# Gate projection of the sparse half put ahead of the first sparse pair's transposes and exponentials

## Chip, cores and metric

The kernel runs on one core of one Trainium2 chip. The metric is the device time of one execution in microseconds (us). In the profile PE is TensorE (PEld its weight loads), ACT ScalarE, DVE VectorE, POOL GpSimd, and SP the engine that issues the plain DMAs.

## What is computed

The reference is a first block (mixers, cross attention, and a feed-forward layer that looks up single-neuron experts) followed by two layers of a second block. All of what is changed lies in the second block:

```python
def hybrid_layer(x, w_in, w_out, ln_g, ln_b, rel_bias, topk):
    proj = jnp.einsum('bsd,dn->bsn', x, w_in)
    qA, kA, vA, gA, qB, kB, vB, gB, qI, kI, wI = jnp.split(proj, SPLIT_POINTS, axis=-1)
    oA = stick_breaking_attention(heads(qA), heads(kA), heads(vA))
    oB = dsa_sparse_attention(heads(qB), heads(kB), heads(vB), qI, kI, wI, rel_bias, topk)
    mix = jnp.concatenate([oA * jax.nn.silu(gA), oB * jax.nn.silu(gB)], axis=-1)
    y = jnp.einsum('bsm,md->bsd', mix, w_out)
    return layer_norm(ALPHA * x + y, ln_g, ln_b)
```

The sequence has 512 tokens of width 1024. Each half (A, the "stick" half, and B, the "sparse" half) has 8 heads of width 64. `gB` is the gate projection of the sparse half: a 1024 by 512 product for each token. The expert look-up of the first block gathers 16 rows for each of 8 heads of each token, and each row is dotted with the token, passed through a GELU, and added.

## The kernel before

The second block is run in three groups of query tiles of 128 tokens: group 0 has tiles 0 and 1, group 1 has tile 2, group 2 has tile 3. Each group goes through both layers, so there are six passes. In the trace they lie at 1630 to 1900 and 1900 to 2165 us (group 0), 2165 to 2430 and 2430 to 2690 us (group 1), and 2690 to 2850 and 2850 to 3013 us (group 2). What comes before 1630 us is the first block.

Beside the passes of groups 0 and 1 runs the background work: the expert look-up for the tokens of the next group, 128 rows for each of the two groups. A row is one gather into one of 10 slots, issued by POOL (L1335, about 1 MB for the 128 tokens), a dot product on DVE (L2438, 1.2 us), and a scaled addition on DVE (L2452, 1.3 us). Four rows make a lot. A lot's GELU (L2252) runs on ACT once its four dots are there, with an activation table load before it and one after it (1.28 us each). DVE multiplies the result by the gate weights (L2444, "weigh") before it adds the rows of the lot, five rows behind the dots. Which rows are done where is fixed: the code of DVE and ACT has named points between its steps (`rows(point)`, `gelus(point)`), and a list of weights, `layer_points`, says how many rows are due at each. From it follow, for the points around the change:

- group 0 layer 0: GELU of lot 9 at the point ("g1", 0), of lot 10 at ("gate1"), of lot 11 at ("sparse", 0, 2). DVE weighs lot 9 in its rows of ("g1", 1) and lot 10 in those of ("gate1").
- group 0 layer 1: GELU of lot 26 at ("gate1"), weighed by DVE in its rows of ("gate1").
- group 1 layer 0: GELU of lot 10 at ("g1", 2), weighed in ("gate1").
- group 1 layer 1: GELU of lot 26 at ("gate1"), weighed in ("gate1").
- group 2 has no background work.

Each engine carries out its program in order and waits on semaphores. A pass has 8 head pairs u: 0 to 3 stick, 4 to 7 sparse. `pair(l, u)` projects queries and keys (L78, weights from the ring), `natural` projects gates or values for a whole half (L2082, 16 matmul instructions of 512 columns for each tile). For a sparse pair, `sparse_logits` (L2159) is followed by `shift` on DVE (L2572: adds the bias, and takes the maximum), `sparse_weights` on ACT (L2350: exponentials, one for each head and tile), `turn_weights` on PE (L2167: transposes), `copy_turned` on ACT (L2357) and `sparse_out` on PE (L78). `gates` on ACT handles a tile's gate projection in four operations: copy, exponential, logarithm, exponential (L2334, L2335, L2337, L2339). `turn_mix` (L2191) and `copy_mix` (L2362) turn the finished half of the mix. Projections share two PSUM banks in turn, so that `pair(l, 6)` waits for the first `copy_mix` of the stick half.

Weights come through a ring of 6 blocks of 512 KB, loaded by SP in the order of use (L1874): ..., v1 (4 blocks), pair 5 (2), g1 (4), pair 6 (2), pair 7 (2), out (8). A block's load waits until the block six before it has been used: the g1 blocks wait for the value projection v1 and need nothing later. Behind the load that waits for g1, SP issues the bias of the third sparse pair (`load_bias(l, 2)`, L1919), which waits also for the first `shift`, and behind the loads that wait for pair 6 the bias of the fourth. POOL adds the mask to each bias (`add_keep`, L2001) before its `shift`.

Of the kernel before, what the change touches and what calls it, by code (L numbers as in the profile page):

```python
# [26 lines left out]
PAIRS = HEADS // 2  # L27
# [1634 lines left out]
STICK, SPARSE = 0, 1  # L1662
# [117 lines left out]
def group_stage(nc, A, m, number, out):  # L1780
# [8 lines left out]
    tiles = GROUPS[number]  # L1789
# [27 lines left out]
    with ctx:  # L1817
# [36 lines left out]
        with nc.Block() as block:  # L1854
# [165 lines left out]
            def _(pe):  # L2020
                def start(job):
                    n = job_at[job]
                    if n >= 2:
                        pe.wait_ge(proj_copied, n - 1)
                    return ps[:, n % 2, :]
# [50 lines left out]
                def natural(l, name, half):  # L2076
                    for t in tiles:
                        bank = start((l, f"{name}{half}", t))
                        for b in range(4):
                            w = weights_of(l, half, name, b)  # L2080
                            for c in range(2):
                                made = nc.tensor.matmul(bank, x_t[:, 2 * b + c, local(t)], w[:, c * HALF:(c + 1) * HALF],  # L2082
                                                        start=b == 0 and c == 0, stop=b == 3 and c == 1)
                        made.then_inc(proj_done, 1)

                def pair(l, u):
                    bank = start((l, "pair", u))
                    for k, name in enumerate("qk"):
                        made = turned_product(bank[:, k * NQ:(k + 1) * NQ], weights_of(l, u // PAIRS, name, u % PAIRS))
                    made.then_inc(proj_done, 1)  # L2090
# [72 lines left out]
                def turn_weights(l, u):  # L2163
                    pe.wait_ge(prob_ready, PAIRS * l + u - PAIRS + 1)
                    for e in range(2):
                        for b in range(SC // P):
                            made = nc.tensor.transpose(ps[:, pair_banks(u) + e, b * P:(b + 1) * P], work[:, u % 2, e, b * P:(b + 1) * P], m.ident[:, :])  # L2167
                    made.then_inc(turned, 1)
# [38 lines left out]
                for l in range(LAYERS):  # L2207
                    for t in tiles:
                        for n in range(2):
                            turn_input(l, t, n)  # L2210
                    copied(("x", last, 1) if l == 0 else (l - 1, "x", last, 1))
                    index_keys(l)
                    index_queries(l, 0)
                    index_queries(l, 1)
                    natural(l, "v", STICK)
                    index_scores(l)
                    pair(l, 0)
                    stick_logits(l, 0)
                    natural(l, "g", STICK)
                    for u in range(PAIRS):  # L2220
                        pair(l, u + 1)
                        tails(l, u)
                        if u + 1 < PAIRS:
                            stick_logits(l, u + 1)
                        else:
                            natural(l, "v", SPARSE)
                            sparse_logits(l, PAIRS)
                        stick_out(l, u)
                    for u in range(PAIRS, UNITS):
                        if u + 1 < UNITS:  # L2230
                            pair(l, u + 1)
                        turn_weights(l, u)
                        if u + 1 < UNITS:
                            sparse_logits(l, u + 1)
                        if u == PAIRS:
                            natural(l, "g", SPARSE)
                        sparse_out(l, u)
                        if u == PAIRS:
                            turn_mix(l, STICK)
                    turn_mix(l, SPARSE)  # L2240
                    output(l)

            @block.scalar
            def _(act):
# [77 lines left out]
                        act.wait_ge(attended, UNITS * l + u)  # L2322
                    nc.scalar.activation(work[:, 1, :, :], ps[:, pair_banks(u):pair_banks(u) + 2, 0:SC], ACT.Exp).then_inc(weighted, 1)

                def gates(l, half, done):

                    if half == STICK and searched:
                        act.wait_ge(summed, SCORES * (l + 1))
                    if half == SPARSE:
                        act.wait_ge(gate_ready, NT * (2 * l + 1))  # L2330
                    for n, t in enumerate(tiles):
                        count = NT * (2 * l + half) + n
                        bank = finished((l, f"g{half}", t))
                        nc.scalar.activation(mix[:, n, half * HALF:(half + 1) * HALF], bank, ACT.Copy)  # L2334
                        nc.scalar.activation(share[:, n, :], bank, ACT.Exp, scale=-1.0).then_inc(proj_copied, 1)  # L2335
                        act.wait_ge(proj_copied, job_at[l, f"g{half}", t] + 1)
                        nc.scalar.activation(share[:, n, :], share[:, n, :], ACT.Ln, bias=1.0).then_inc(gate_step, 1)  # L2337
                        act.wait_ge(gate_step, 2 * count + 1)
                        nc.scalar.activation(share[:, n, :], share[:, n, :], ACT.Exp, scale=-1.0).then_inc(gate_step, 1)  # L2339
                        done = gelus((l, f"g{half}", t), done)  # L2340
                    return done

                def sparse_weights(l, u):
                    n = PAIRS * l + u - PAIRS
# [20 lines left out]
                done = 0  # L2365
# [4 lines left out]
                done = gelus((0, "first"), done)  # L2370
                inverse_roots(0)
                for l in range(LAYERS):
                    done = gelus((l, "first"), done)
                    for t in tiles:
                        for n in range(2):
                            copy_input(l, t, n)
                    done = gelus((l, "start"), done)
                    copy_index_keys(l)
                    done = gelus((l, "kI"), done)
                    for n in range(2):  # L2380
                        copy_index_queries(l, n)
                        done = gelus((l, "qI", n), done)
                    done = copy_values(l, STICK, done)
                    for n in range(SCORES):
                        rectify(l, n)
                        if n % 2:
                            done = gelus((l, "scores", searched[n // HEADS], n % HEADS), done)
                    copy_pair(l, 0)
                    done = gelus((l, "pair0"), done)
                    softplus(l, 0)  # L2390
                    done = gelus((l, "soft0"), done)
                    done = gates(l, STICK, done)
                    for u in range(PAIRS):
                        copy_pair(l, u + 1)
                        done = gelus((l, "stick", u, 0), done)
                        stick_weights(l, u)
                        done = gelus((l, "stick", u, 1), done)
                        if u + 1 < PAIRS:
                            softplus(l, u + 1)
                        else:  # L2400
                            done = copy_values(l, SPARSE, done)
                        done = gelus((l, "stick", u, 2), done)
                        done = gelus((l, "stick", u, 3), done)
                    done = gelus((l, "keep"), done)
                    for u in range(PAIRS, UNITS):
                        p = u - PAIRS
                        if p == 0:
                            sparse_weights(l, u)
                            copy_pair(l, u + 1)
                            copy_turned(l, u)  # L2410
                            done = gates(l, SPARSE, done)
                            done = gelus((l, "gate1"), done)
                            copy_mix(l, STICK)
                        else:
                            sparse_weights(l, u)
                            done = gelus((l, "sparse", p, 0), done) if p else done
                            if u + 1 < UNITS:
                                copy_pair(l, u + 1)
                            copy_turned(l, u)
                        done = gelus((l, "sparse", p, 1), done)  # L2420
                        done = gelus((l, "sparse", p, 2), done)
                        done = gelus((l, "sparse", p, 3), done)
                    copy_mix(l, SPARSE)
                    done = gelus((l, "out"), done)
                    inverse_roots(l + 1)
                    done = gelus((l, "norm"), done)
# [355 lines left out]
```

## Time and profile before

| | |
|---|---|
| time, median of 3 runs | 3016.38 us (3012.67 to 3020.07) |
| the profiled execution: time, span | 3014.64 us, 3012.9 us |
| busy: PE, DVE, POOL, ACT | 81%, 58%, 32%, 30% of the span |
| gathers of expert rows (software queue) | 536.90 MB of 803.85 MB moved |
| TensorE clock granted, mean | 0.888 |

The profiled execution is 1.7 us below the median. The busy shares are averages over stages that have different limits: the passes of groups 0 and 1 have the gathers and VectorE's rows beside them, those of group 2 have not. In a timeline row stand the start, the duration, engine, line, operation, output and inputs, and in brackets the idle time of the engine before it and what ended it. For DVE rows "issue" names a wait that the profile can't attribute.

### The profile page before, as it was taken

Reading aid. Unit: us, or ns where it says so; the run is one execution under the profiler, and the core shown is the slowest. Engines: PE = TensorE matmul, PEld = TensorE weight load, DVE = VectorE, ACT = ScalarE, POOL = GpSimd, SP = SyncE. Lnnn points to the kernel's source line nnn. Section 1 sums busy time; section 2 is a strip of 40 time slices with the busy share of each in tenths; the row PEclk is TensorE's granted clock in tenths of the full one; section 3 lists DMA queues with packets and bytes.
Section 4 is the critical chain, followed back from the end, with each engine's and each line's share of the span. In section 5 each row is a group of like instructions: output and inputs, shape, how many; then the busy total and the mean of one; then the engine's idle time right before and its main releaser. Section 6 shows DMA issues by size and latency. Waiting matters only on the chain. (4 is left out here: it accounts for less than half of the span.)

```text
span 3012.9 us, 30208 instructions
## 1 busy us (share of the span) xinstructions
PE 2428.3 (81%) x9721; PEld 1627.9 (54%) x9721; DVE 1743.7 (58%) x3652; ACT 905.9 (30%) x1730; POOL 979.0 (32%) x691
## 2 busy tenths in 40 slices
PE   6997999869876888889785996798557468559897
PEld 4776878758653343334333664575246336436674
DVE  3444311031128888988964687587669859855142
ACT  4444222223311222222222442244134324323232
POOL 2232554433302434343451234234213523410001
PEclk9998999979988999999897997898778677769899
DMA  4321333223118999999998899899789999964553
GB/s 159 94 66 49 98 105 97 101 71 108 56 39 330 392 418 409 411 412 403 403 416 351 320 366 369 331 355 402 277 342 382 413 400 373 390 269 157 215 185 138
DMA packets 255851, 803.85 MB, mean 267 GB/s; under 512 B 18302, under 2 KB 138518, under 8 KB 190183
## 3 DMA queue, kind: packets, MB, share of 16 engines
q0 software_dynamic: 73728, 536.90, 43.9%
q1 hardware_dynamic: 181991, 265.35, 25.3%
q8 instruction: 63, 1.03, 0.1%
q14 instruction: 69, 0.57, 0.0%
HBM read 793.36 MB, written 14.07 MB: 268 GB/s over the span
## 5 line engine op out<-in xcount | busy, mean ns | idle before, releaser
L1335 POOL DMA_INDIRECT gathered<-in_peer_rows,experts x436 | 530.6, 1217 | 928.8 <-DVE x_res L2452 630.7
L1446 PE MATMUL peer_banks<-gathered,peer_diags 128*128 128x512 f32 x720 | 342.8, 633 | 60.3 <-ACT peer_diags L1506 60.2
L78 PE MATMUL group_banks<-group_x_t,group_ring 128*128 128x128 f32 (+1 forms) x2016 | 340.2, 332 | 15.9 <-ACT group_x_t L2264 8.4
L2438 DVE CUSTOM_DVE_ANT_0 gathered<-gathered,late_nat 128x1024 f32<-128x1024 f32 x256 | 315.7, 1236 | 42.0 <-DMA gathered<-in_peer_rows,experts 29.0
L78 PEld LDWEIGHTS group_banks<-group_x_t,group_ring 128*128 128x128 f32 x2016 | 307.6, 208 | 46.0 <-ACT group_x_t L2264 10.8
L2452 DVE SCALAR_TENSOR_TENSOR x_res<-gathered,group_weights,x_res 128x1024 f32<-128x1024 f32 x256 | 329.8, 1288 | 2.5
L1446 PEld LDWEIGHTS peer_banks<-gathered,peer_diags 128*128 128x128 f32 x720 | 144.6, 204 | 249.5 <-issue 249.2
L2082 PE MATMUL group_banks<-group_ring,group_x_t 128*128 128x512 f32 x512 | 233.3, 610 | 28.2 <-DMA group_ring<-in_weights 28.2
L1609 DVE CUSTOM_DVE_ANT_0 peer_product<-gathered,early_nat 128x1024 f32<-128x1024 f32 x180 | 214.8, 1222 | 41.2 <-DMA gathered<-in_peer_rows,experts 41.1
L1446 PE MATMUL peer_banks<-peer_early_gathered,peer_diags 128*128 128x512 f32 x304 | 148.9, 643 | 45.9 <-ACT peer_diags L1506 45.9
L1499 ACT ACTIVATE peer_acts<-peer_dots 128x2 f32<-128x2 f32 x128 | 26.0, 203 | 518.1 <-DVE peer_dots L1609 517.9
L2082 PEld LDWEIGHTS group_banks<-group_ring,group_x_t 128*128 128x128 f32 x512 | 98.1, 197 | 150.0 <-issue 117.7
L2001 POOL TENSOR_TENSOR group_bias<-group_bias,group_keep 128x768 f32<-128x768 f32 (+1 forms) x24 | 48.9, 2049 | 342.9 <-DVE group_keep L2507 249.6
L1335 POOL DMA_INDIRECT peer_early_gathered<-in_peer_rows,experts x76 | 81.6, 1074 | 207.0 <-PE peer_banks L1446 119.1
L1446 PEld LDWEIGHTS peer_banks<-peer_early_gathered,peer_diags 128*128 128x128 f32 x304 | 61.9, 208 | 127.8 <-issue 127.8
L2167 PE MATMUL group_banks<-ident,group_work 128*128 128x128 f32 x160 | 30.0, 342 | 121.5 <-ACT group_work L2350 115.6
L2200 PE MATMUL group_banks<-group_ring,group_mix_t 128*128 128x512 f32 x256 | 123.7, 646 | 4.1 <-ACT group_mix_t L2362 4.1
L78 PE MATMUL peer_banks<-peer_h_t,peer_w 128*128 128x512 f32 x256 | 115.2, 605 | 8.0 <-DMA peer_w<-in_w_pq 8.0
L95 POOL TENSOR_TENSOR mixer_wq_parts<-mixer_wq,mixer_wq_parts 128x1024 fp32r<-128x1024 f32 x24 | 58.2, 2427 | 189.4 <-ACT mixer_wq_parts L526 121.9
L78 PEld LDWEIGHTS group_banks<-group_values,group_work 128*128 128x128 f32 x640 | 93.5, 229 | 24.1 <-ACT group_work L2357 16.9
L944 DVE TENSOR_TENSOR merge_gated<-merge_gates,merge_banks 128x512 f32<-128x512 f32 x16 | 11.0, 689 | 163.1 <-PE merge_banks L78 163.1
L2043 PE MATMUL group_banks<-ident,x_res 128*128 128x128 f32 x64 | 16.2, 427 | 107.2 <-DVE x_res L2476 81.4
(324 smaller groups left out, 4307.9 us busy)
## 6 DMA issues: line engine op xcount, KB each, us to landing
group_ring<-in_weights SPq DMA_DIRECT2D x270, 512.0 KB, 5.5
mixer_wq<-in_w_in SPq DMA_DIRECT2D x24, 512.0 KB, 4.4
mixer_wk<-in_w_in SPq DMA_DIRECT2D x24, 512.0 KB, 5.7
peer_w<-in_w_pq SPq DMA_DIRECT2D x8, 1024.0 KB
gathered<-in_peer_rows,experts POOLq DMA_INDIRECT x436
diff_wv<-in_w_in SPq DMA_DIRECT2D x8, 512.0 KB, 4.2
conv_wb<-in_w_in SPq DMA_DIRECT2D x8, 512.0 KB, 4.1
merge_w<-in_w_conv_out SPq DMA_DIRECT2D x8, 512.0 KB, 3.6
```

Source lines behind the costliest of these rows:

```text
L78: last = nc.tensor.matmul(out, lhsT, rhs, start=n == 0, stop=n == len(pairs) - 1)
L95: return engine.tensor_tensor(low, whole, high.bitcast(F32), ALU.subtract)
L1335: nc.gpsimd.indirect_dma_start(row_buffer(m, r), None, A["peer_rows"], bass.IndirectOffsetOnAxis(ap=at, axis=0))\
L1446: last = nc.tensor.matmul(ps[:, ACC[unit % 2] + half, :], diags[:, r % DIAGS, :], row_buffer(m, r)[:, D + half * BANK:D + (half + 1) * BAN ...
L1499: nc.scalar.activation(acts[:, lot % RING, :], dots[:, lot % RING, :], ACT.Gelu).then_inc(gelu_done, 1)
L1609: nc.vector.tensor_tensor_reduce(out=product[:, r % 2, :], in0=row_buffer(m, r)[:, 0:D], in1=nat[t // 2][:, t % 2, :], scale=1.0, scalar=0 ...
L2001: nc.gpsimd.tensor_tensor(bias[:, n % 2, :, :], bias[:, n % 2, :, :], keep[:, :].unsqueeze(1).to_broadcast([P, 2, SC]), ALU.add)\
L2082: made = nc.tensor.matmul(bank, x_t[:, 2 * b + c, local(t)], w[:, c * HALF:(c + 1) * HALF], start=b == 0 and c == 0, stop=b == 3 and c == 1)
L2167: made = nc.tensor.transpose(ps[:, pair_banks(u) + e, b * P:(b + 1) * P], work[:, u % 2, e, b * P:(b + 1) * P], m.ident[:, :])
L2200: made = nc.tensor.matmul(ps[:, 2 + 2 * n + half, :], mix_t[:, c, local(t)], w[:, half * HALF:(half + 1) * HALF], start=c == 0, stop=c == ...
L2438: nc.vector.tensor_tensor_reduce(out=row, in0=row, in1=m.late_nat[:, t % 2, :], scale=1.0, scalar=0.0, op0=ALU.mult, op1=ALU.add, accum_ou ...
L2452: nc.vector.scalar_tensor_tensor(out=m.x[:, t, :], in0=row_buffer(m, r)[:, D:2 * D], scalar=weights[:, lot % bg.RING, n % bg.LOT:n % bg.LO ...
```

## The change

In a pass, TensorE now runs the gate projection of the sparse half right after `pair(l, 5)`, before `turn_weights` of pair 4. ScalarE copies pair 5 and does the gates of all tiles before the exponentials of pair 4. `gates` no longer calls `gelus` behind each tile: for the stick half the calls follow behind the loop, and for the sparse half the GELUs due at ("g1", t) are done by the call for ("gate1"), behind `copy_turned` of pair 4. DVE, POOL and SP have the same programs as before.

```diff
                     for u in range(PAIRS, UNITS):
                         if u + 1 < UNITS:
                             pair(l, u + 1)
+                        if u == PAIRS:
+                            natural(l, "g", SPARSE)
                         turn_weights(l, u)
                         if u + 1 < UNITS:
                             sparse_logits(l, u + 1)
-                        if u == PAIRS:
-                            natural(l, "g", SPARSE)
                         sparse_out(l, u)
                         if u == PAIRS:
                             turn_mix(l, STICK)
@@
-                def gates(l, half, done):
+                def gates(l, half):
...
                         nc.scalar.activation(share[:, n, :], share[:, n, :], ACT.Exp, scale=-1.0).then_inc(gate_step, 1)
-                        done = gelus((l, f"g{half}", t), done)
-                    return done
@@
                     done = gelus((l, "soft0"), done)
-                    done = gates(l, STICK, done)
+                    gates(l, STICK)
+                    for t in tiles:
+                        done = gelus((l, "g0", t), done)
@@
                         if p == 0:
+                            copy_pair(l, u + 1)
+                            gates(l, SPARSE)
                             sparse_weights(l, u)
-                            copy_pair(l, u + 1)
                             copy_turned(l, u)
-                            done = gates(l, SPARSE, done)
                             done = gelus((l, "gate1"), done)
                             copy_mix(l, STICK)
```

## Rows read from the trace of the kernel before

**Rows 1.** Windows, one per pass; the last three columns are clock, DMA share, GB/s

```profile
1630.00:1900.00 270.00, 224.94 (x856) 153.18 (x856) 192.15 (x325) 91.90 (x157) 88.73 (x65) 0.88 0.92 354
...
2165.00:2430.00 265.00, 151.89 (x728) 108.96 (x728) 202.99 (x315) 85.27 (x131) 90.93 (x67) 0.75 0.92 363
...
2850.00:3013.00 163.00, 141.15 (x784) 100.94 (x784) 54.99 (x106) 44.49 (x80) 9.35 (x4) 0.93 0.45 167
```

**Rows 2.** Waits of VectorE in 1630 to 2690: us in total, times, longest

```profile
DVE group_weights L2444 <- ACT group_acts L2252: 64.0, 8, 21.0
...
DVE gathered L2438 <- DMA gathered<-in_peer_rows,experts: 29.0, 25, 2.9
```

**Rows 3.** Timeline, group 0 layer 0, first half

```profile
1782.84 0.40 ACT L2350 ACTIVATE group_work<-group_work,group_neg_top 128x128 f32<-128x128 f32 x1 [6.07 <-DVE group_neg_top L2572]
...
1784.76 0.88 PE L2167 MATMUL group_banks<-ident,group_work 128*128 128x128 f32 x6 [2.12 <-ACT group_work L2350]
...
1785.68 0.81 ACT L2357 ACTIVATE group_work<-group_banks 128x768 f32<-128x768 f32 x1 [0.44 <-PE group_banks L2167]
...
1792.02 8.85 PE L2082 MATMUL group_banks<-group_ring,group_x_t 128*128 128x512 f32 x20 [0.17 <-DMA group_ring<-in_weights]
...
1798.06 0.16 DVE L2444 TENSOR_TENSOR group_weights<-group_acts,gates 128x4 f32<-128x4 f32 x1 [7.33 <-ACT group_acts L2252]
...
1800.91 0.60 ACT L2334 ACTIVATE group_mix<-group_banks 128x512 f32<-128x512 f32 x1 [1.58 <-PE group_banks L2082]
...
1806.80 5.41 PE L78 MATMUL group_banks<-group_x_t,group_ring 128*128 128x256 f32 x16 [3.76 <-ACT group_mix_t L2362]
```

**Rows 4.** Timeline, group 0 layer 0, second half

```profile
1811.78 1.23 DVE L2438 CUSTOM_DVE_ANT_0 gathered<-gathered,late_nat 128x1024 f32<-128x1024 f32 x1 [2.64 <-DMA gathered<-in_peer_rows,experts]
...
1817.02 1.85 SPq L1919 DMA_DIRECT2D group_bias<-bias_table  x4
...
1842.84 1.80 POOL L2001 TENSOR_TENSOR group_bias<-group_bias,group_keep 128x768 f32<-128x768 f32 x1 [9.44 <-DMA group_bias<-bias_table]
...
1844.77 0.29 DVE L2572 CUSTOM_DVE_ANT_0 group_work<-group_banks,group_bias 128x128 f32<-128x128 f32 x1 [8.07 <-POOL group_bias L2001]
```

**Rows 5.** Timeline, group 0 layer 1

```profile
2055.33 0.88 PE L2167 MATMUL group_banks<-ident,group_work 128*128 128x128 f32 x6 [3.11 <-ACT group_work L2350]
...
2076.63 0.16 DVE L2444 TENSOR_TENSOR group_weights<-group_acts,gates 128x4 f32<-128x4 f32 x1 [7.68 <-ACT group_acts L2252]
```

**Rows 6.** DMA issues, 2043 to 2054, median us to landing

```profile
group_ring<-in_weights SPq DMA_DIRECT2D x6, 512.0 KB, 18.9
```

**Rows 7.** Windows, group 0 layer 1, columns as in Rows 1

```profile
2055.30:2059.30 4.00, 3.97 (x16) 2.42 (x17) 3.96 (x8) 1.32 (x3) 1.21 (x1) 0.61 1.01 417
```

**Rows 8.** Timeline, group 1 layer 0

```profile
2344.18 1.54 PE L2167 MATMUL group_banks<-ident,group_work 128*128 128x128 f32 x6 [16.27 <-ACT group_work L2350]
...
2359.64 0.16 DVE L2444 TENSOR_TENSOR group_weights<-group_acts,gates 128x4 f32<-128x4 f32 x1 [3.79 <-ACT group_acts L2252]
```

**Rows 9.** Timeline, group 1 layer 1

```profile
2606.69 0.16 DVE L2444 TENSOR_TENSOR group_weights<-group_acts,gates 128x4 f32<-128x4 f32 x1 [3.83 <-ACT group_acts L2252]
```

**Rows 10.** Timeline, group 2 layer 1

```profile
2944.45 0.72 ACT L2350 ACTIVATE group_work<-group_work,group_neg_top 128x512 f32<-128x512 f32 x1 [1.21 <-DVE group_neg_top L2572]
...
2945.79 0.19 ACT L2350 ACTIVATION_READ_ACCUMULATOR group_work<-group_work,group_neg_top 128x1 f32 x1
...
2958.32 0.60 ACT L2334 ACTIVATE group_mix<-group_banks 128x512 f32<-128x512 f32 x1 [7.16 <-PE group_banks L2082]
...
2960.10 0.63 ACT L2339 ACTIVATE group_share<-group_share 128x512 f32<-128x512 f32 x1
...
2972.74 1.09 PE L2167 MATMUL group_banks<-ident,group_work 128*128 128x128 f32 x8 [1.16 <-ACT group_work L2350]
...
2975.15 0.69 DVE L2572 CUSTOM_DVE_ANT_0 group_work<-group_banks,group_bias 128x512 f32<-128x512 f32 x1 [3.40 <-PE group_banks L2159]
```

**Rows 11.** Timeline, group 2 layer 0

```profile
2815.25 1.09 PE L2167 MATMUL group_banks<-ident,group_work 128*128 128x128 f32 x8 [1.07 <-ACT group_work L2350]
```

## The prediction

> **What bounds the kernel now.** I read the passes one by one first. In the four passes of groups 0 and 1 TensorE is busy for 152 to 225 of some 265 us, VectorE for 192 to 203, and the DMA engines for about 0.9 of the time at 350 to 360 GB/s; in the two of group 2 TensorE is busy for 141 of 163 us and the rest has room [rows 1]. So the same edit meets two machines. In groups 0 and 1 the chain runs mostly through VectorE, which has its rows in order between the steps of the pass, and behind it stand the gathers. VectorE's idle time there is the second view: 64.0 us in 8 waits go to GELU results (L2444), 29.0 us in 25 waits to gathers that have not landed [rows 2]. In group 2 TensorE's own program is the chain. The third view is the timeline around the moved work, pass by pass, and there the question is the same each time: what did TensorE do in the place where the gate projection (g1) is put, and who waits for ScalarE behind the gates.
>
> **The change, part by part.** No arithmetic is added or removed: g1 is 16 matmul instructions for each tile before and after. In group 0 layer 0, two table switches fall away because two lots' GELUs are now done in one call. ScalarE isn't short of time there, so this is costed at nothing; if it were, it is two loads of 1.28 us. The gates of the stick half do the same work in the same order in all six passes (the first tile of two has no lot due), so nothing.
>
> *Group 2, layer 1.* TensorE has no hole here: the exponentials of pair 4 end at 2944.45 to 2945.98 [rows 10], before pair 5 is through at about 2949, and the transposes follow without a wait. With the change g1 takes that place, and then the transposes wait for ScalarE, which now first does the gates: from g1's end to the first gate operation 0.26 us, the four gate operations 2.41 us (2958.32 to 2960.73), the exponentials 1.53 us, 0.05 us to TensorE [rows 10]. That is 4.25 us of new idle time. The copy of the transposes, once hidden under g1, is hidden under the next logits but for some 0.1 us. Given back: TensorE waited 1.16 us before the transposes of pair 6, because the third bias came late [rows 10]; that bias is now asked for some 2 us earlier, since g1 ends earlier, and TensorE comes 4.25 us later, so the wait goes. Net +3.1 us. What is late next is the fourth bias, which SP issues only when pair 6 is through, 4.25 us later; the last shift began at 2975.15 right behind it [rows 10]. If it lands as slowly as before, +4.3; it competes with fewer blocks, so I keep 3.1.
>
> *Group 2, layer 0.* Same pattern, with 1.07 us given back [rows 11]: +3.2 us. Bounds for each of the two passes: 1.7 (the last shift also had slack) and 4.3.
>
> *TensorE's clock in group 2.* In group 0 layer 1 TensorE idled 3.11 us before the transposes [rows 5], and in the 4 us behind it the granted clock was 0.61, so near the lower level of 1.2 GHz for most of it [rows 7]; that is 0.39 times 4 = 1.6 us lost. The new gap of 4.25 us is longer. I charge 1.6 us twice, 3.2 in all; bounds 0 (the gap falls well) and 6.4 (the low clock comes back later in the pass as well). The Trainium skill says in "TensorE: Matmul & The Clock Gate", section "HAM oscillation", that idle gaps of some length put the array back to the lower clock, so that the burst behind each gap starts slow. By that rule the whole of the 3.2 us is due, and without it nothing; the trace of group 0 layer 1 agrees with the rule.
>
> *Group 0, layer 0.* TensorE idled only 2.12 us before the transposes, and the last g1 block landed at 1792.02 [rows 3]. So g1 can start earlier but not end earlier: its first tile waits for the same block, and its second tile is through at 1800.7, as before. Now the order on ScalarE costs. Before, the GELU of lot 9 stood between the gates of the two tiles, and VectorE, which had waited for it for 7.33 us, went on at 1798.06 [rows 3]. After, it stands behind the gates of both tiles (1800.91 + 2.41 = 1803.3), the exponentials (1782.84 to 1784.76, so 1.92: 1805.2), transposes and their copy (1784.76 to 1786.49, so 1.73: 1807.0) [rows 3], and a table load and the GELU (1.5): 1808.5. VectorE goes on 10.5 us later. Behind it lot 10 must be done as well before `copy_mix`: two additions, two dots and a weigh, 5.2 us, then GELU and table load, so `copy_mix` comes at 1815.3 and pair 6 at about 1816 where it was at 1806.80 [rows 3]. VectorE gets back the 2.64 us that it waited for a gather: +7.9 on that road [rows 4]. But the fourth bias is issued behind pair 6 (at 1817.02), POOL waited 9.44 us for its landing, and VectorE 8.07 us for POOL [rows 4]: on that road +9.3. I take +9. Below 5 it can't well come, since both roads would have to be shortened by the DMA queues emptying during VectorE's longer stall; above, 10.5.
>
> *Group 0, layer 1.* One lot (26), which stands behind the gates in both orders, so only the exponentials, transposes and copy (1.92 + 1.73 = 3.7) are put ahead of it, less what g1 gains. TensorE idled 3.11 us [rows 5]. A block takes 18.9 us to land [rows 6]; the g1 blocks are issued at about 2044, so the last is there at about 2063, and g1 gains 1 to 2 us at most. Range −2.7 (blocks there at once) to +3.3; I take +2. VectorE waited 7.68 us for this lot [rows 5], so it is on the path.
>
> *Group 1, both layers.* Here is the hole that fits: TensorE idled 16.27 us before the transposes in layer 0 [rows 8] and about as long in layer 1, because the shift on VectorE is late. g1 fits into it, and the gates are done before the exponentials are asked for. But what follows is not TensorE's. The next exponentials wait for VectorE's rows; the only wait of VectorE that hangs on the moved work is that for a GELU behind the gates, 3.79 and 3.83 us [rows 8, 9]. It goes. In its place the gathers are late next: the DMA engines are at 0.92 of the pass [rows 1], and VectorE waits for gathers already [rows 2]. I take half, −2 in each pass; bounds 0 and −3.8.
>
> **Sum.** 9 + 2 − 2 − 2 + 3.1 + 3.2 + 3.2 = +16.5 us on the profiled execution's own 3014.6: 3031.1. The median before is 1.7 us above that execution. I leave the forecast at 3031.
>
> **Rivals.**
>
> *B, TensorE's holes are the gain.* g1 leaves TensorE's chain wherever it idled: 2.12 and 3.11 in group 0 [rows 3, 5], and g1's whole length of about 7.5 us in each pass of group 1 [rows 8]. With group 2 at no cost that is −20, 2996 us. For it: the holes are real, and waits for exponentials end them. Against: behind them VectorE's rows, not TensorE, end the next wait. It decides if in group 1 the shift of pair 5 turns out to wait for its logits, and not to stand behind rows. This is the one that ends on the other side.
>
> *C, the loss is absorbed.* The delays of group 0 fall to the lower bounds (5 and −2.7), since queues that emptied deliver faster, group 1 gives its full 7.6, and group 2 costs 2 × 1.7 with no slow clock: 5 − 2.7 − 7.6 + 3.4 = −1.9, and half way to the forecast it is +7. So 3013 to 3023, about no change. For it: in the trace VectorE has 29 us of gather waits that a late VectorE would not meet. Against: only the 2.64 us lies close behind the delay in group 0.
>
> *D, the low clock spreads.* Upper bounds: 10.5 + 3.3 + 0 + 8.6 + 6.4 = +29, 3044 us. For it: TensorE gets new gaps in four passes. Against: the clock came back within 4 us behind the gap that I can see.
>
> **How the numbers follow.** No change within 0.3% (about what a measurement of this kernel can tell apart) is within 9 us of 3016.4. Chances: forecast 0.50, C 0.24, D 0.20, B 0.06. So slower 0.70, the same 0.24, faster 0.06. The range reaches from the upper part of C to most of D: 3016 to 3043.
>
> **What the profile after would show.** Right: in group 2 an idle time of about 4.2 us before the first transposes of pair 4, ended by ScalarE; no wait before those of pair 6; in group 0 layer 0 VectorE waiting about 18 us for the GELU of lot 9 where it waited 7.33; in group 1 the waits of 3.8 us at L2444 gone, with more waiting for gathers, and the waits of 16 us before the transposes smaller by g1. Wrong: if group 1's passes are shorter by more than 4 us each, VectorE was not their bound; if group 0 layer 0 is not longer, the GELU's place doesn't matter; if group 2 is not longer, ScalarE's gates overlap something that I took for serial.

## The result and the profile after

The changed kernel takes 3028.62 us (median of 6 runs, 3023.45 to 3035.45), the kernel before 3018.2 us (median of 6, 3012.67 to 3022.36). The ratio is 1.004, with a 95% interval of 1.0027 to 1.0052: slower by 12 us (10.4 us by the medians alone), and 8 to 16 us are in the interval. Further down, one execution of e6 is left out of its ratio: it took 3267.69 us at a mean granted clock of 0.76, the others of that kernel had 0.88 to 0.89. The profiled execution took 3027.14 us, with a span of 3025.4 us where the one before had 3012.9. The first lines of its page, engines and then the queue of the gathers, hardly differ from before: the work is the same, and 12.5 us more are waits and work at a lower clock. The mean granted clock doesn't show it (0.891 after, 0.888 before).

```profile
PE 2431.9 (80%) x9721; PEld 1632.8 (54%) x9721; DVE 1746.1 (58%) x3652; ACT 903.6 (30%) x1728; POOL 987.5 (33%) x691
...
q0 software_dynamic: 73728, 536.90, 43.8%
```

**Group 2.** This is the timeline of layer 1 after, which answers to [rows 10].

```profile
2950.85 7.03 PE L2082 MATMUL group_banks<-group_ring,group_x_t 128*128 128x512 f32 x16
...
2957.98 0.60 ACT L2334 ACTIVATE group_mix<-group_banks 128x512 f32<-128x512 f32 x1 [6.48 <-PE group_banks L2082]
...
2961.85 1.27 PE L2167 MATMUL group_banks<-ident,group_work 128*128 128x128 f32 x8 [3.97 <-ACT group_work L2348]
...
2963.05 2.08 PE L2159 MATMUL group_banks<-group_k_t,group_q_t 64*128 64x512 f32 x4
...
2965.06 3.68 PE L78 MATMUL group_banks<-group_values,group_work 128*128 128x64 f32 x16
...
2967.20 2.36 POOL L2001 TENSOR_TENSOR group_bias<-group_bias,group_keep 128x1024 f32<-128x1024 f32 x1 [21.50 <-DMA group_bias<-bias_table]
...
2969.38 5.41 PE L78 MATMUL group_banks<-group_x_t,group_ring 128*128 128x128 f32 x32
...
2974.62 1.04 PE L2167 MATMUL group_banks<-ident,group_work 128*128 128x128 f32 x8
...
2982.23 1.04 PE L2167 MATMUL group_banks<-ident,group_work 128*128 128x128 f32 x8
...
2987.57 1.09 PE L2167 MATMUL group_banks<-ident,group_work 128*128 128x128 f32 x8 [1.19 <-ACT group_work L2348]
```

The projection runs from 2950.85 to 2957.9. ScalarE's gates start at 2957.98, and the transposes of pair 4 begin at 2961.85 after 3.97 us of idle time (forecast 4.25). POOL has the third bias ready at 2969.6, and the transposes of pair 6 (2982.23) no longer wait. Those of pair 7 (2987.57) wait 1.19 us, though, where they waited 0.51 before:

```profile
2977.46 1.09 PE L2167 MATMUL group_banks<-ident,group_work 128*128 128x128 f32 x8 [0.51 <-ACT group_work L2350]
```

This is the fourth bias, which the prediction had named as late next: POOL has it ready at 2985.14, and the last shift begins at 2985.26. So in layer 1 some 0.7 of the 1.16 us given back are taken again. Layer 0 has the same pattern up to pair 6: 3.97 us before the transposes at 2801.20, none before those at 2821.60. There the last wait went down, from 1.76 to 0.32 us.

What the reader should look at are the durations in between: logits 2.08 us where they take 1.13 at full clock, the product 3.68 for 2.00, the projection of pair 6 5.41 for 3.79. The windows of the same stretch say why (columns as in Rows 1, the clock third from the end):

```profile
2954.00:2957.90 3.90, 3.88 (x10) 1.38 (x8) 0.00 (x0) 0.00 (x0) 0.00 (x0) 1.00 0.39 152
2961.80:2967.00 5.20, 5.15 (x21) 3.33 (x22) 1.82 (x5) 1.02 (x1) 0.00 (x0) 0.58 0.78 307
2967.00:2974.60 7.60, 7.60 (x45) 7.60 (x45) 0.09 (x1) 2.00 (x5) 2.36 (x1) 0.61 0.00 1
```

From the first transposes to those of pair 5 it is 12.77 us after (2961.85 to 2974.62). In the trace before, the same stretch was 14.75 us with the projection in it (from 2949.06 to 2963.81), so 7.78 without its 6.97. The 5.0 us on top are work at or near the lower clock of 1.2 GHz, but for the 0.3 us of copy that is no longer hidden (e4 below has 8.06 us for the same stretch at full clock).

**Group 0, layer 0.** The same rows as in [rows 3]:

```profile
1779.71 14.16 PE L2082 MATMUL group_banks<-group_ring,group_x_t 128*128 128x512 f32 x32
...
1793.90 0.60 ACT L2334 ACTIVATE group_mix<-group_banks 128x512 f32<-128x512 f32 x1 [4.40 <-PE group_banks L2082]
...
1798.12 1.04 PE L2167 MATMUL group_banks<-ident,group_work 128*128 128x128 f32 x6 [4.25 <-ACT group_work L2348]
...
1801.55 0.16 DVE L2444 TENSOR_TENSOR group_weights<-group_acts,gates 128x4 f32<-128x4 f32 x1 [11.59 <-ACT group_acts L2252]
...
1808.72 8.95 PE L78 MATMUL group_banks<-group_x_t,group_ring 128*128 128x256 f32 x32 [3.52 <-ACT group_mix_t L2360]
```

The projection of both tiles runs from 1779.71 to 1793.87 without a stop of its own. The fourth block did land only when TensorE came to it: its first weight load waited for it (0.82 us, of which the products lost at most 0.3: the row takes 14.16 us, and 13.90 in e4 and e9).

```profile
1785.01 0.19 PEld L2082 LDWEIGHTS group_banks<-group_ring,group_x_t 128*128 128x128 f32 x1 [0.82 <-DMA group_ring<-in_weights]
```

I had taken the landing at 1792.02 in [rows 3] for a fixed time. Measured from the end of the value projection, which frees the ring (1773.3 before, 1770.5 after), the block was there after 18.8 us in the trace before and after 14.5 us in this one. So the projection is over 4.2 us earlier than before by the same measure, and VectorE's wait at L2444 is 11.59 us, not the 18 us forecast, where it was 7.33. The landing differs from trace to trace. These are from e3, then e8 (below), which have TensorE's new order in group 0 as well:

```profile
1788.85 8.85 PE L2082 MATMUL group_banks<-group_ring,group_x_t 128*128 128x512 f32 x20 [1.79 <-DMA group_ring<-in_weights]
```

```profile
1789.91 8.85 PE L2082 MATMUL group_banks<-group_ring,group_x_t 128*128 128x512 f32 x20 [1.80 <-DMA group_ring<-in_weights]
```

There the block came 17.8 and 16.8 us after the value projection, and TensorE stood still for the ring for 3.0 and 2.0 us in all. In e4 and e9 it didn't wait.

The trace before was also not typical in the place where the projection was put. Of six traces whose code is as before in group 0 (before, e1, e2, e5, e6, e10), two have a hole of 2.1 us before the first transposes, and four have one of 4.1 us, as e1, whose wait for the GELU of lot 9 comes second:

```profile
1780.16 0.88 PE L2167 MATMUL group_banks<-ident,group_work 128*128 128x128 f32 x6 [4.10 <-ACT group_work L2353]
...
1794.65 0.16 DVE L2453 TENSOR_TENSOR group_weights<-group_acts,gates 128x4 f32<-128x4 f32 x1 [8.52 <-ACT group_acts L2254]
```

The logits behind this hole run slowly (1.63 us where they took 0.93), and the projection ends 30.8 us after the value projection, not 27.6 as in the trace before. Against such an execution the new place of the projection gains 7.4 us, not 4.2.

**Group 1.** Waits of VectorE over both passes; before (2164.4 to 2678.6 us) first:

```profile
DVE group_weights L2444 <- ACT group_acts L2252: 28.7, 3, 21.0
DVE gathered L2438 <- DMA gathered<-in_peer_rows,experts: 23.7, 20, 2.9
```

and after (2167 to 2677.1 us):

```profile
DVE gathered L2438 <- DMA gathered<-in_peer_rows,experts: 26.5, 29, 2.7
DVE group_weights L2444 <- ACT group_acts L2252: 22.5, 1, 22.5
```

Two of the three waits for a GELU (3.79 and 3.83 us) are gone, as forecast, and 9 more short waits for gathers stand in their place. And the projection did not simply drop into the idle time: in layer 0 it had to wait for its own weights.

```profile
2333.76 7.08 PE L2082 MATMUL group_banks<-group_ring,group_x_t 128*128 128x512 f32 x12 [2.64 <-DMA group_ring<-in_weights]
...
2341.58 1.98 PE L2082 MATMUL group_banks<-group_ring,group_x_t 128*128 128x512 f32 x4 [0.73 <-DMA group_ring<-in_weights]
...
2347.50 0.88 PE L2167 MATMUL group_banks<-ident,group_work 128*128 128x128 f32 x6 [3.94 <-ACT group_work L2348]
...
2373.21 1.54 PE L2167 MATMUL group_banks<-ident,group_work 128*128 128x128 f32 x6 [15.30 <-ACT group_work L2348]
```

It stood still twice for the ring, ended at 2343.56, and the gates behind it held the transposes until 2347.50, where before they began at 2344.18 [rows 8] (the whole trace is 2.5 us later there). The transposes of pair 5 still wait 15.30 us: they hang on VectorE's rows. In the trace before that wait was 9.19 us, so part of the hole has only moved from pair 4 to pair 5.

Lengths of whole passes from one trace each can't size these effects. From the end of layer 0's output product to the end of layer 1's, group 0 took 266.7 us in the trace before and 272.4 us in that of experiment e1, whose code is the same there. The experiments therefore change one group at a time and are timed.

### The profile page after: what moved, and what is told of

Its sections match the earlier page's. It is cut to its first block and busy times, and to the rows that moved or that the text cites. A ratio compares the mean times of both kernels' runs of the same rounds, so it can differ in the third digit from the quotient of the medians.

```text
span 3025.4 us, 30206 instructions
## 1 busy us (share of the span) xinstructions
PE 2431.9 (80%) x9721; PEld 1632.8 (54%) x9721; DVE 1746.1 (58%) x3652; ACT 903.6 (30%) x1728; POOL 987.5 (33%) x691
## 5 line engine op out<-in xcount | busy, mean ns | idle before, releaser
L2167 PE MATMUL group_banks<-ident,group_work 128*128 128x128 f32 x160 | 28.7, 331 | 116.3 <-ACT group_work L2348 116.2
L78 PE MATMUL group_banks<-group_values,group_work 128*128 128x64 f32 x640 | 102.7, 325 | 6.1 <-ACT group_work L2355 5.8
## 6 DMA issues: line engine op xcount, KB each, us to landing
peer_w<-in_w_pq SPq DMA_DIRECT2D x8, 1024.0 KB, 17.8
```

Of the source, the lines that this page charges most:

```text
L78: last = nc.tensor.matmul(out, lhsT, rhs, start=n == 0, stop=n == len(pairs) - 1)
```

## The experiments

All ratios are to the kernel before, with runs on the same chip, and 95% intervals. e1 to e4, e5 to e8 and e9 to e12 ran on three different chips. In the edits `number` is the group. All kernels but e5 do the work of the kernel before, in another order.

### e1, e2, e3: the whole reorder in one group only

```diff
+                        if u == PAIRS and number == 2:      # e2: 1, e3: 0
+                            natural(l, "g", SPARSE)
                         turn_weights(l, u)
...
-                        if u == PAIRS:
+                        if u == PAIRS and not (number == 2):
                             natural(l, "g", SPARSE)
...
-                            sparse_weights(l, u)
-                            copy_pair(l, u + 1)
-                            copy_turned(l, u)
-                            done = gates(l, SPARSE, done)
+                            if number == 2:                 # e2: 1, e3: 0
+                                copy_pair(l, u + 1)
+                                done = gates(l, SPARSE, done, late=True)   # no GELUs between tiles
+                                sparse_weights(l, u)
+                                copy_turned(l, u)
+                            else: ...                       # as before
```

> The whole reorder in group 2 only. Theory (the order costs idle time plus the low clock behind it): in each of the two passes 4.0 us of idle time before the transposes, 4 to 5 us of work at the lower clock behind it, 1.1 us given back: +8 us for each pass, +16 in all, less or more 3 us for where the low clock falls at the passes' ends; so +12 to +18 us, ratio 1.004 to 1.006, more than the whole change. Rival (the clock's cost is made up within the pass, only the idle time counts): +6 us, ratio 1.002. Rival (group 2 is not where it is lost): within 3 us.

Measured: 1.0039 (1.002 to 1.0058), +12 us. The loss of the whole change is in group 2. That is at the lower edge of what was expected, and the rival's 1.002, in which only the idle time counts, is just at the edge of the interval; the slow stretches in the traces, and e5, speak against it. One reason is in the trace: in layer 1 the stretch from pair 4's to pair 5's transposes took 9.52 us there and not 12.77, because the clock came back sooner (0.67 was granted in the first 5.2 us of it, 0.50 in layer 0); in layer 0 it took 12.53. Added up over both passes of this trace, 7.9 us of idle time, 6.5 us on top of the stretches' 7.78, and 2.8 us less waiting before pairs 6 and 7 make 11.6 us.

> The whole reorder in group 1 only. Theory (only VectorE's 3.8 us wait goes, and gathers are late in its place): -2 us for each pass, -4 in all, ratio 0.9985 to 0.999. Rival (TensorE's idle 16 us are the gain there): -15 us, ratio 0.995. Rival (earlier weight loads hold up the gathers): 0 to +3 us, as layer 0 seemed to show (+3.3 us by the two traces).

Measured: 0.9985 (0.997 to 0.9999), −4.5 us. The theory's −4 holds; the 15 us of TensorE's idle time are excluded, and so, narrowly, is a loss. In its trace VectorE has one wait for a GELU in group 1 (22.7 us), not three, and 28 for gathers.

> The whole reorder in group 0 only. Theory (GELUs stand behind gates, exponentials and copy): by the two traces +1.9 us in layer 0 and +3.0 us in layer 1, so +5 us, ratio 1.0015. As predicted before the result: +11 us, ratio 1.0035. Rival (absorbed by gather waits): 0.

Measured: 1.0002 (0.9986 to 1.0018). The +11 us of the prediction are excluded. The reading from the two traces (+5) is just inside the interval, no change is in its middle. The execution that was traced was one of the slowest (3030.33 us, the median is 3016.98), and in it the forecast's picture did come: the block late, VectorE's weigh of lot 9 34.5 us after the value projection (forecast 35.2, and 24.8 in the trace before). The three groups add up to +8 us (11.8 − 4.5 + 0.6), with intervals of ±4 to ±6 us each; the whole change had +12.

### e4: TensorE's part alone, in all groups

```diff
+                        if u == PAIRS:
+                            natural(l, "g", SPARSE)
                         turn_weights(l, u)
                         if u + 1 < UNITS:
                             sparse_logits(l, u + 1)
-                        if u == PAIRS:
-                            natural(l, "g", SPARSE)
```

> Only TensorE's part: the gate projection is put before the transposes in all passes, ScalarE keeps the order of before (exponentials, copy of pair 5, copy of the transposes, gates with their GELUs). Theory (ScalarE's order makes the loss): no idle time before the transposes in group 2, no low clock behind it, the wait of 1.1 us for the third bias gone: -2 us there; group 1 -3 us, group 0 0 to +3 us (the GELUs stand behind both tiles' projections and the copy). In all -5 to +1 us, ratio 0.998 to 1.000. Rival (TensorE's order makes the loss): as the whole change, 1.004.

Measured: 0.9965 (0.995 to 0.9979), −10.6 us: faster than the kernel before, and 20 us or so faster than the change as made. The sign of the whole change is set by what ScalarE does. The two short waits of VectorE for a GELU in group 1 are gone here too (22.7 us in one wait, against 28.7 in three before), so TensorE's earlier projection alone is enough for that, without ScalarE's new order. TensorE in group 2, layer 1:

```profile
2939.01 7.03 PE L2082 MATMUL group_banks<-group_ring,group_x_t 128*128 128x512 f32 x16
2945.88 1.04 PE L2167 MATMUL group_banks<-ident,group_work 128*128 128x128 f32 x8
...
2948.12 1.97 PE L78 MATMUL group_banks<-group_values,group_work 128*128 128x64 f32 x16
...
2953.94 1.04 PE L2167 MATMUL group_banks<-ident,group_work 128*128 128x128 f32 x8
```

No wait before the transposes (2945.88), and 8.06 us to the next ones (2953.94), all at full clock.

### e5: the idle time filled

```diff
+                        if u == PAIRS and number == 2:
+                            for _ in range(4):
+                                nc.tensor.matmul(ps[:, pair_banks(u + 1), :], m.ident[:, :],
+                                                 values[STICK][:, 0, :], start=True, stop=True)
                         turn_weights(l, u)
```

Added to e1, between projection and transposes; the next logits overwrite the bank.

> The whole reorder in group 2 only, as in e1, and four more 128x512 products (their result is overwritten) on TensorE between the gate projection and the transposes, 3.4 us, where e1 has 3.97 us of idle time. Nothing gets shorter but the idle time's length; the chain through ScalarE is the same. Theory (the low clock behind the idle time costs about 4.9 us in each pass, more than the idle time itself): the clock stays at its upper level and the pass of e1 gets shorter by 3 to 5 us, so -6 to -10 us against e1, ratio to before 1.001 to 1.002. Rival (the idle time on the path is all that counts): as e1, 1.004.

Measured: 1.0014 (1.0 to 1.0028), against 1.0039 for e1: −7.5 us for added work. The two ratios are from different chips and their intervals overlap (1.002 to 1.0028), so the size is uncertain by some 7 us; what happened is seen best in the trace, though it is of the slowest of the 12 executions (3030.13 us). The timeline of layer 1 and two windows:

```profile
2964.71 3.60 PE L2236 MATMUL group_banks<-group_values,ident 128*128 128x512 f32 x8
2968.84 1.09 PE L2167 MATMUL group_banks<-ident,group_work 128*128 128x128 f32 x8 [0.53 <-ACT group_work L2356]
...
2971.14 1.97 PE L78 MATMUL group_banks<-group_values,group_work 128*128 128x64 f32 x16
...
2973.39 3.74 PE L78 MATMUL group_banks<-group_x_t,group_ring 128*128 128x128 f32 x32
2976.96 1.04 PE L2167 MATMUL group_banks<-ident,group_work 128*128 128x128 f32 x8
```

```profile
2968.80:2974.00 5.20, 5.01 (x38) 4.05 (x39) 1.91 (x5) 1.44 (x2) 0.00 (x0) 1.00 0.80 306
2974.00:2977.00 3.00, 3.00 (x29) 3.00 (x29) 0.00 (x0) 1.59 (x5) 2.28 (x1) 1.00 0.03 7
```

The four products take 3.60 us, 0.53 us of idle time are left, the granted clock stays at 1.00, and the stretch is 8.12 us in both layers. It was 12.79 and 12.77 in the changed kernel and 12.53 and 9.52 in e1. So the low clock cost 4.7 us in the dearest of these passes, more than the idle time in front of it, and 1.4 us in the cheapest. The wait for ScalarE is the same as in e1, since filler and rest make 4.13 us.

### e6: exponentials first, gates before the copy of the transposes

```diff
                             if number == 2:
+                                sparse_weights(l, u)
                                 copy_pair(l, u + 1)
                                 done = gates(l, SPARSE, done, late=True)
-                                sparse_weights(l, u)
                                 copy_turned(l, u)
```

> Group 2 only: TensorE's new order, and on ScalarE the exponentials first, then the copy of pair 5 and the gates, then the copy of the transposes. The transposes do not wait then; the output product of the first sparse pair does, for what the gates (2.41 us), the start (0.26 us) and the copy (1.02 us) are longer than transposes and logits (2.02 us): 1.7 us of idle time in place of 3.97, in each pass. Theory: +1.7 us, less 1.1 us for the third bias, with a gap too short for the low clock: 0 to +2 us in all, ratio 1.000 to 1.0007. Rival (any new gap at this place brings the low clock): +8 us, 1.0027.

Measured: 1.002 (1.0007 to 1.0033), +6 us, near the rival's +8 and above the theory's 0 to +2 (which the lower end of the interval, +2.1, just excludes). The theory fell on the clock:

```profile
2954.16 1.04 PE L2167 MATMUL group_banks<-ident,group_work 128*128 128x128 f32 x8
...
2956.73 1.01 ACT L2360 ACTIVATE group_work<-group_banks 128x1024 f32<-128x1024 f32 x1
...
2957.88 2.71 PE L78 MATMUL group_banks<-group_values,group_work 128*128 128x64 f32 x16 [1.63 <-ACT group_work L2360]
...
2965.34 1.04 PE L2167 MATMUL group_banks<-ident,group_work 128*128 128x128 f32 x8
```

```profile
2957.80:2961.80 4.00, 3.92 (x23) 3.95 (x24) 0.42 (x1) 0.32 (x1) 0.00 (x0) 0.64 0.88 338
```

The copy of the transposes starts only behind the gates, the product waits 1.63 us as worked out, and the 4 us behind this short gap were granted 0.64 (0.66 in layer 0). The stretch is 11.18 us: 1.6 us of gap and 1.5 us of low clock over the 8.06 of e4. Two passes of 3.1 us make the 6 us measured; e10 (below), which has the order of e4 in this group, stood at 1.0.

### e7: TensorE's order in all groups, ScalarE's new order in group 1 only

```diff
-                            if number == 2:
+                            if number == 1:
```

(with TensorE's order of e4)

> TensorE's new order in all groups; ScalarE's new order only in group 1, where TensorE idles 16 us. Theory (in group 1 both orders on ScalarE hide behind VectorE's late shift): the same as e4, ratio 0.9965, within 3 us. Rival (the gates must be done before the shift there to give group 1's gain): faster than e4 by 3 us or more, 0.9955.

Measured: 0.9984 (0.9969 to 0.9999). This was slower than e4's 0.9965, but on another chip, and the intervals overlap. So both went to one chip again (e11, e12).

### e8: TensorE's part in group 0 only

```diff
+                        if u == PAIRS and number == 0:
+                            natural(l, "g", SPARSE)
                         turn_weights(l, u)
...
-                        if u == PAIRS:
+                        if u == PAIRS and not (number == 0):
                             natural(l, "g", SPARSE)
```

> TensorE's new order in group 0 only, ScalarE as before. The whole reorder in group 0 gave no change (e3, 1.0002). Theory (TensorE's earlier projection gains some us there, and ScalarE's order, GELUs behind it all, gives them back): faster than before by 3 to 6 us, ratio 0.998 to 0.999. Rival (group 0 does not care about either): 1.000, and the 9 us of e4 come from group 1 and group 2.

Measured: 0.9986 (0.9971 to 1.0001), −4.2 us, just short of being told from nothing. It fits the theory, and the hole of 4.1 us that four of the six traces with the old order have; the rival isn't excluded by this run alone.

### e9: group 0 with the GELU between the tiles' gates again

```diff
-                                done = gates(l, SPARSE, done, late=True)
+                                done = gates(l, SPARSE, done, late=False)
```

(in e3)

> The whole reorder in group 0 only, as in e3, but the GELU of lot 9 stands between the gates of the two tiles again (lot 10 stays behind the copy of the transposes). Theory (the GELU's place makes VectorE's wait in layer 0): VectorE's wait for the GELU of lot 9, 15.0 us in the trace of e3, goes down to 5 us or less, and the time against before is 0.998 to 1.000, at most 6 us better than e3. Rival (group 0's time hangs on the gathers, not on this wait): the wait goes and the time stays at 1.000.

Measured: 0.9984 (0.997 to 0.9997), where e3 had 1.0002: 5.5 us better. VectorE's weigh of lot 9 in e3's trace, and then in e9's:

```profile
1805.57 0.16 DVE L2453 TENSOR_TENSOR group_weights<-group_acts,gates 128x4 f32<-128x4 f32 x1 [15.01 <-ACT group_acts L2254]
```

```profile
1790.27 0.16 DVE L2453 TENSOR_TENSOR group_weights<-group_acts,gates 128x4 f32<-128x4 f32 x1 [0.84 <-ACT group_acts L2254]
```

15.01 us of wait against 0.84 us. Some 3 us of the difference are the late block in e3's trace (the changed kernel, without that, waits 11.59). The reading is that ScalarE's queue order costs group 0 about 5 us, that TensorE's order gives back about as much, and that this is why e3 shows nothing. (The two ratios are from different chips and their intervals overlap, 0.9986 to 0.9997, so the shorter wait is shown, the 5 us are not.)

### e10: TensorE's part in group 2 only

```diff
+                        if u == PAIRS and number == 2:
+                            natural(l, "g", SPARSE)
                         turn_weights(l, u)
...
-                        if u == PAIRS:
+                        if u == PAIRS and not (number == 2):
                             natural(l, "g", SPARSE)
```

> TensorE's new order in group 2 only, ScalarE as before. Theory: the gate projection costs the same on TensorE in either place, the copy of the transposes hides but for some tenths of a microsecond, and the wait of 1.1 us for the third bias goes: -2 to 0 us in both passes together, ratio 0.9993 to 1.000. Rival (a part of the gain of e4 is here): 0.9985 or less.

Measured: 1.0 (0.9989 to 1.0011). The moved projection costs and gives nothing in group 2. The gain of e4 is in groups 0 and 1.

### e11, e12: e4 and e7 on one chip

> The kernel of e4 on one chip with that of e7. Theory (they do the same, and the difference between 0.9965 and 0.9984 was the chip or chance): both between 0.996 and 0.9985, and within 3 us of each other. Rival: e4's kernel is faster by 5 us or more here too.

> The kernel of e7 beside that of e4, on one chip: within 3 us of it by the theory, 5 us or more slower by the rival.

Measured: 0.9968 (0.9955 to 0.998) and 0.9971 (0.9956 to 0.9986), medians 3007.88 and 3009.78 us. They do the same; in group 1 ScalarE's order makes no difference that can be seen. The faster version is TensorE's part alone, twice measured at −10 us.

## Why the prediction was right, and where it was not

The forecast was slower, 3031 us; measured were 3028.6. The direction and the size came out, but two terms of the sum were off, in opposite directions. That the sum landed so near is in part luck: two thirds of it (+11 of 16.5) were for group 0, where e3 shows +0.6, and group 2 alone makes up the +12 that were measured.

- **Idle time in group 2** (forecast 4.25 us in each pass, measured 3.97) and the third bias's wait of 1.1 us given back: right, step by step, but for the last shift, which made the transposes of pair 7 wait 0.7 us longer in layer 1. The 0.3 us less is two short starts: the gates began 0.1 us behind the projection's end, and the first exponential 0.1 us before the last gate operation had ended. (The 0.26 us of the forecast were counted from the start of the next product, 2958.06; from the projection's end before, 2958.22, it was 0.1 us as well.)
- **TensorE's clock in group 2** (forecast 1.6 us in each pass): mis-sized. It cost 4.4 to 4.7 us in three of the four passes that were traced, and 1.4 us in the fourth (e1, layer 1), against e5. The row that I used had a gap of 3.11 us with the clock at 0.61 for 4 us [rows 7]. Behind 3.97 us of gap it was at 0.58 for 5.2 us and at 0.61 for 7.6 us more. The rule of the Trainium skill ("TensorE: Matmul & The Clock Gate", section "HAM oscillation"), that a long gap makes the burst behind it start slow, is borne out by e5, where the filled gap left the clock at 1.00. But e6's gap of 1.63 us had a slow stretch behind it as well, so here the length of one gap isn't all that counts. The section's own case is one of DMA waits; here it was another engine's queue.
- **Group 2 in all**: forecast +9.5 us, measured +12 (6 to 17.5; e1).
- **Group 0, layer 0** (forecast +9): wrong. The step that failed is "g1 can start earlier but not end earlier: its first tile waits for the same block". The landing at 1792.02 was one draw: the block came 14.5 us after the value projection in the trace after, 16.8 to 18.8 us in those of e8, e3 and before. In the trace of e3, where it was late, the chain on ScalarE ran to within 1 us as forecast (34.5 us to the weigh against 35.2); in the trace after the projection ended 4.2 us earlier, and against the four traces with the longer hole 7.4 us earlier. The order on ScalarE cost VectorE a wait of 11.59 us after and 15.01 in e3 (7.33 and 8.5 with the old order), and the projection's earlier end offset it. e8 and e9 put both parts at about 4 to 5 us for the group as a whole, neither clear of noise.
- **Group 0, layer 1** (forecast +2): not measured by itself. Group 0 in all was +0.6 us (−4 to +5) against a forecast of +11.
- **Group 1** (forecast −4): right, −4.5 us (e2), and by the mechanism named: the waits for GELUs went, waits for gathers came. By e4 the projection's earlier end is enough for the first. Not foreseen was that the weights would stop the projection in layer 0.
- **Rival B** (TensorE's holes are the gain, −20 us) is excluded by e2. It was nearer to the truth of e4 than I had allowed: with ScalarE left alone, TensorE's move does win 10 us, in groups 0 and 1.
- **Rival C** (absorbed) held for group 0, and **rival D** (the low clock spreads) for group 2.

What stays open: how the 10 us of e4 split over group 1's GELU waits, its exponentials and group 0. The single parts (−4.5, −4.2, 0) add up to −9, each with an uncertainty of about 4 us. It is also open why the low clock near the end of a pass comes in some traces and not in others: from the last transposes to the end of the output product it was 25.3 us in layer 0 and 22.1 in layer 1 before, and 22.1 and 24.5 after.

## What to carry to other kernels

When work is moved into a hole of one engine, ask what its consumer does with it: the projection cost TensorE nothing in its new place, but the four gate operations that follow it on ScalarE went ahead of exponentials and a GELU that two other engines waited for. Move the producer alone first, and leave the consumer's queue in the order in which others wait. In a stage where TensorE itself is the chain, price a new gap of a few microseconds at the gap plus the slow work behind it, which here was the larger part in three passes of four. And the landing time of a transfer, or the length of a hole, that one trace shows isn't fixed: look at a second trace before a term of some microseconds is hung on it.

## What the hardware showed that I had not expected

Four added products of 128x512, 3.6 us of work for nothing, took the kernel from 1.0039 to 1.0014 (7.5 us, uncertain by about as much), and the granted clock stayed at 1.00 where it had been 0.50 to 0.67 for the work behind. A gap of only 1.63 us was followed by 4 us at 0.64 (e6), while one of 2.12 us in group 0 layer 0 before was followed by logits at full speed (0.93 us), one of 1.76 us in group 2 layer 0 before by 8.8 us at 0.50, and the two passes of e1 with the same gap of 3.97 us lost 4.5 us and 1.5 us. In these traces a gap's cost is a draw from a range, not a number.
